# Four delta-rule heads computed on unnormalised keys and queries, with the next head's whole q projection moved ahead of the output transposes

## What is computed

```
conv = sum(src[:, j:j + T] * conv_w[j] for j in range(CONV_W))       # width 4, on q, k, v
qa, ka, va = jnp.split(jax.nn.silu(conv), 3, axis=-1)
qa = l2_normalize(qa) * HEAD_DIM_A ** -0.5
ka = l2_normalize(ka)
log_a = -exp(a_log) * softplus(a_raw + dt_bias);  beta = sigmoid(b_raw)
G = cumsum(g);  decay = exp(where(causal, G_i - G_j, -inf))          # per chunk
a_mat = where(strict, (k beta) @ k^T * decay, 0)
wu = triangular_solve(eye + a_mat, [k beta exp(G), v beta])
qk = (q @ k^T) * decay;  qg = q * exp(G);  kd = k * exp(G_last - G)
# scan over chunks
v_new = u - w @ S;  o = qg @ S + qk @ v_new;  S = S * g_last + kd^T @ v_new
o_a = rms_norm(o_a, gnorm_a) * silu(z)
```

## Time and profile before

| | us |
|---|---|
| median of 3 runs | 1989.44 |
| lowest, highest | 1988.54, 1991.89 |
| the profiled execution | 1989.23 |
| its span in the trace | 1987.2 |
| TensorE busy | 1910.3 |
| mean granted clock, share of full | 0.981 |

### The profile page before, as it was taken

How to read it: one execution, slowest core, us unless ns; L and a number is a source line. 1 busy time by engine, 2 the same in 40 slices (tenths; PEclk the granted TensorE clock), 3 DMA queues, 4 the chain that set the end, 5 groups by cost and what they waited for, 6 DMA issues and landing times.

```text
span 1987.2 us, 29633 instructions
## 1 busy us (share of the span) xinstructions
PE 1910.3 (96%) x12298; PEld 1855.4 (93%) x12298; DVE 755.8 (38%) x1525; ACT 619.8 (31%) x1335; POOL 559.3 (28%) x332
## 2 busy tenths in 40 slices
PE   6899999999999999999989999999999999999998
PEld 6898998999999899988989999999999999999997
DVE  5552552552452312332346424641252145115413
ACT  5532342342342323334424323321231023103311
POOL 1241141131131110211114434531343234214431
PEclk9999999989999999999989999999999999999999
DMA  5312312312312432444554332221121122112212
GB/s 155 87 52 62 98 51 59 102 46 64 94 53 86 143 105 94 148 132 145 181 171 146 98 87 75 84 65 43 53 90 49 43 66 84 43 53 74 64 53 88
DMA packets 235839, 173.25 MB, mean 87 GB/s; under 512 B 16277, under 2 KB 225250, under 8 KB 235322
## 3 DMA queue, kind: packets, MB, share of 16 engines
q1 hardware_dynamic: 200586, 131.57, 22.4%
q10 hardware_dynamic: 35120, 39.80, 6.1%
HBM read 134.04 MB, written 47.72 MB: 91 GB/s over the span
## 4 chain that ended last, share of the span: by engine, by line
PE 81%; DVE 8%; ACT 4%; DMA 4%; issue 2%; POOL 1%; SPq 0%; DVEq 0%; ACTq 0%; POOLq 0%
PE dense L207 50%; PE dense L232 13%; PE work L1359 1%; PE work L1371 1%; PE work L995 1%; PE work L1005 1%; DVE systems L853 1%; PE work L1409 1%; PE work L207 1%; PE work L1392 1%; PE work L1351 1%; PE work L935 1%; PE work L1003 1%; PE work L962 1%; PE work L410 1%
## 5 line engine op out<-in xcount | busy, mean ns | idle before, releaser
L196 POOL TENSOR_TENSOR WL<-Wraw,WH 128x1024 fp32r<-128x1024 f32 (+1 forms) x131 | 315.3, 2407 | 1075.2 <-ACT WH L191 1075.1
L207 PE MATMUL dense<-hH,WH 128*128 128x352 f32 x1392 | 456.0, 328 | 5.5 <-POOL WL L196 5.5
L207 PE MATMUL dense<-hL,WH 128*128 128x352 f32 x1392 | 450.7, 324 | 0.0
L207 PE MATMUL dense<-hH,WL 128*128 128x352 f32 x1392 | 450.3, 324 | 0.0
L232 PE MATMUL dense<-hH,WH 128*128 128x352 f32 x744 | 268.8, 361 | 5.6 <-ACT fill L241 5.3
L207 PEld LDWEIGHTS dense<-hH,WH 128*128 128x128 f32 x1392 | 265.0, 190 | 6.9 <-POOL WL L196 5.7
L207 PEld LDWEIGHTS dense<-hL,WH 128*128 128x128 f32 x1392 | 265.1, 190 | 0.0
L207 PEld LDWEIGHTS dense<-hH,WL 128*128 128x128 f32 x1392 | 264.6, 190 | 0.0
L207 PE MATMUL dense<-gH,WH 128*128 128x352 f32 x768 | 247.5, 322 | 2.5 <-DVE gL L1754 1.7
L191 ACT ACTIVATE WH<-Wraw 128x1024 fp32r<-128x1024 f32 (+1 forms) x131 | 136.3, 1041 | 363.7 <-PE dense L207 296.3
L207 PE MATMUL dense<-gL,WH 128*128 128x352 f32 x768 | 247.8, 323 | 0.0
(11 more groups left out here) (318 smaller groups left out, 2652.0 us busy)
## 6 DMA issues: line engine op xcount, KB each, us to landing
Wraw<-in_w_in SPq DMA_DIRECT2D x51, 512.0 KB, 4.2
Wraw<-in_w_up SPq DMA_DIRECT2D x32, 512.0 KB, 4.0
Wraw<-in_w_down SPq DMA_DIRECT2D x32, 512.0 KB, 3.6
cache<-in_cache_win SPq DMA_DIRECT2D x20, 512.0 KB, 6.3
qkv_scratch<-fill ACTq DMA_DIRECT2D x54, 176.0 KB, 1.8
raw<-qkv_scratch SPq DMA_DIRECT2D x6, 1584.0 KB, 9.2
out_win_s<-in_cache_win ACTq DMA_DIRECT2D x16, 512.0 KB, 4.1
gb_scratch<-fill ACTq DMA_DIRECT2D x24, 176.0 KB, 2.5
```

Of the source, the lines that this page charges most:

```text
L196: G.tensor_tensor(WL[:, s, 0:k], Wraw[:, s, 0:k], WH[:, s, 0:k].bitcast(F32), ALU.subtract).then_inc(sem("w_split"), 1)
L207: ins = PE.matmul(out[:, 0:TN], w[:, s, k0 + k, :], x[:, k, cols], start=(k == 0 and i == 0), stop=(k == nk - 1 and i == 2))
```

## The change

Keys and queries stay unnormalised. kk and qk are taken from `qkv` itself, so nothing is transposed back: q is never transposed forward. The key norm enters as `rk2` (1 over the sum of squares, from ScalarE squares with accumulation over the transposed k in PSUM) in `at` and in the eviction of v_new, and as its root in `cvb` for v; q's norm enters at the end, in the output's mean (`qeps`, from nine one-column matmuls on `sqq`). exp(G) times q is made without transposes: ScalarE takes Exp of the broadcast `cum_b`, GpSimd multiplies by q (`qg`). Operations are regrouped: kbg and kd are made in 128x512 products from PSUM. All own jobs are issued as parts, the fills are dealt out anew, and for h < 3 the whole q projection (t = 0, 1, 2) of the next head stands ahead of the output transposes. The diff, cut:

```diff
 def head_tensor(pe, h):
-    for j in range(4):
-        for t in range(NG):
-            if j or (h and t):
-                job(pe, N_HEAD + j, N_HEAD + j + 8 * h, t)
...
-    fill_parts(0, 8)
...
+    proj(1, 0, 24)
+    proj(2, 0, 8)
+    if h == 0:
+        ab_tensor(pe)
+    proj(2, 8, 16)
+    pe.wait_ge(sem("silu"), 3 * h + 2)
+    pe.wait_ge(sem("oa_part"), 3 * h + 1)
+    for i, (lo, hi) in enumerate(((0, 4), (4, 8), (8, 9))):
+        for t in range(lo, hi):
+            c, n = tokens[t]
+            ins = PE.transpose(work[2 + i][0:n, P * (t - lo):P * (t - lo) + P], qkv[:, 1, c:c + n], ident[:, :])
+        ins.then_inc(sem("k_turned"), 1)
+    proj(2, 16, 24)
+    for i in (0, 1, 4, 2, 3):
+        if i == 4:
+            pe.wait_ge(sem("ev_v"), 3 * h + 3)
+            pe.wait_ge(sem("squared"), 3 * h + 3)
...
+            ins = PE.matmul(work[i][0:n, o:o + 2 * n].rearrange("p (x i) -> p x i", x=2), qkv[:, 1, c:c + n], qkv[:, 0:2, c:c + n], start=True, stop=True)
+    proj(3, 0, 17)
     pe.wait_ge(sem("conv_done"), 3 * h + 3)
+    pe.wait_ge(sem("at_made"), h + 2)
...
+    proj(3, 17, 21)
...
+    proj(3, 21, 24)
+    fill_parts(0, 8)
+    pe.wait_ge(sem("sq_q"), h + 1)
+    for t in range(NT9):
+        ins = PE.matmul(work[4][:, t:t + 1], sqq[:, P * t:P * t + P], ones[:, 0:1], start=True, stop=True)
+    fill_parts(8, 20)
-    fill_parts(27, 28)
+    fill_parts(20, 28)
-    fill_parts(28, 29)
+    fill_parts(28, 31)
-    fill_parts(29, 72)
+    fill_parts(31, 44)
-        fill_parts(72 + 2 * s, 73 + 2 * s)
+        fill_parts(44 + 4 * s, 46 + 4 * s)
-        fill_parts(73 + 2 * s, 74 + 2 * s)
+        fill_parts(46 + 4 * s, 48 + 4 * s)
-    scanned = (80, 83, 86, 88, 90, 92, 94, 96)
+    scanned = (60, 65, 69, 74, 78, 83, 87, 92)
-    job(pe, N_HEAD, N_HEAD + 8 + 8 * h, 0)
+    for t in range(NG if h < NH - 1 else 1):
+        job(pe, N_HEAD, N_HEAD + 8 + 8 * h, t)
     pe.wait_ge(sem("o_normed"), h + 1)
-def back(pe, h, t):
...
 def head_pool(pool, h):
...
+    pool.wait_ge(sem("silu"), 3 * h + 1)
+    G.tensor_tensor(qg[:], qg[:], qkv[:, 0], ALU.mult).then_inc(sem("emb_made"), 1)
+    pool.wait_ge(sem("at_made"), h + 2)
...
+    lvl(0)
+    lvl(1)
+    split(5)
+    pool.wait_ge(sem("v_turned"), 3 * h + 3)
+    lvl(2)
 def head_scalar(act, h):
+    def exps():
+        act.wait_ge(sem("e_arg"), h + 1)
+        A.activation(qg[:], cum_b[:], ACT.Exp)
...
 def head_vector(dve, h):
+    conv_of(0)
+    if h:
+        decays()
+    else:
+        ab_rows(dve)
+    conv_of(1)
...
+    for t, (c, n) in enumerate(tokens):
+        ins = V.scalar_tensor_tensor(out=at[0:n, t, 0:n], in0=x, scalar=rk2[0:n, t:t + 1], in1=emb[0:n, t, 0:n], op0=ALU.mult, op1=ALU.mult)
+    ins.then_inc(sem("at_made"), 1)
+    conv_of(2)
```

More of the change, by code:

```diff
@@ L572, in head_sync @@
                 sp.dma_start(sc_in[24:28, j, :], a["conv_w"][0][:, bass.ds(j * WA + h * HD, HD)]).then_inc(sem("sc_loaded"), 16)
-            for j in range(2, 6):
+            for j in range(2, 4):
                 load(j)
@@ L602, in split @@
                 split_lo(pool, N_HEAD + j, N_HEAD + j + 8 * h)
-            for j in range(2, 6):
-                split(j)
+            split(2)
+            if h == 0:
+                split(3)
+                split(4)
             pool.wait_ge(sem("e_ready"), h + 1)
@@ L658, in head_scalar @@
[L658 to L665, removed]
@@ new lines, in head_scalar @@
+            if h:
+                for t in range(NG):
+                    q_out(act, h, 0, t)
+            split(2)
+            q_out(act, h, 1, 0)
+            q_out(act, h, 1, 1)
+            if h:
+                exps()
+            q_out(act, h, 1, 2)
+            split(3)
+            silu(act, h, 0)
+            if h == 0:
+                ab_rows_out(act)
+            else:
+                act.wait_ge(sem("ss_done"), h)
+            act.wait_ge(sem("silu"), 3 * h + 1)
+            A.activation(sqq[:, 0:T], qkv[:, 0, :], ACT.Square).then_inc(sem("sq_q"), 1)
@@ new lines, in head_scalar @@
+            q_out(act, h, 2, 2)
+            split(4)
+            act.wait_ge(sem("mean"), NT9 + 2 * h + 1)
+            A.activation(nk[:], ssk[:], ACT.Sqrt).then_inc(sem("root"), 1)
+            act.wait_ge(sem("oa_part"), 3 * h + 1)
+            for t in range(NG):
+                done(act, N_HEAD + 3 + 8 * h, t)
+                A.activation(silz[:, TN * t:TN * t + TN], dense[t][:, 0:TN], ACT.Silu).then_inc(sem(f"d_free{t}"), 1)
+                if t == 0:
+                    silu(act, h, 2)
@@ L763, in head_vector, with conv_of @@
                 V.memset(pre[:, s, 0:3], 0.0)
-            for j in range(3):
+            def conv_of(j):
                 s = j % 2
@@ L925, in head_tensor, with proj @@
-            fill_parts(0, 8)
+            def proj(j, first, last):
+                for p in range(first, last):
+                    part(pe, N_HEAD + j, N_HEAD + j + 8 * h, p)
+            pe.wait_ge(sem("sc_loaded"), 96 * h + 96)
+            pe.wait_ge(sem("s0_new"), h + 1)
+            pe.wait_ge(sem("ab_read"), 3)
+            apart(pe)
+            for x in range(3):
+                ins = PE.transpose(work[4][:, 28 * x:28 * x + 28], sc_in[:, x], ident[0:28, 0:28])
+            ins.then_inc(sem("sc_turned"), 1)
@@ L930, in head_tensor @@
             ins.then_inc(sem("tails_turned"), 1)
-            pe.wait_ge(sem("squared"), 2 * h + 2)
-            for x in range(2):
-                for t in range(NT9):
-                    ins = PE.matmul(work[4][:, NT9 * x + t:NT9 * x + t + 1], sq[:, x, P * t:P * t + P], ones[:, 0:1], start=True, stop=True)
+            proj(3, 17, 21)
+            pe.wait_ge(sem("silu"), 3 * h + 3)
+            for i, (lo, hi) in enumerate(((0, 4), (4, 8), (8, 9))):
+                for t in range(lo, hi):
+                    c, n = tokens[t]
+                    o = P * (t - lo) if i < 2 else P
+                    ins = PE.transpose(work[(0, 1, 4)[i]][0:n, o:o + P], qkv[:, 2, c:c + n], ident[:, :])
+                ins.then_inc(sem("v_turned"), 1)
```

310 lines of the change are left out of this document (134 added, 176 removed).

## The result

The changed kernel takes 2019.09 us (median of 4 executions, 2016.89 to 2019.82) against 1988.99 of the kernel before: ratio 1.0149, 95% interval 1.0131 to 1.0166. It is slower by 1.5%, +30 us where I forecast +5, and above my range. Its profiled execution has a span of 2015.0 us, 27.8 more than before.

The account below looks back on a forecast made before the run. TensorE, busy for 96% of the span, was taken as the bound. Removed work and old clock drops against new waits and clock drops gave +4.9 each in heads one and three, +2.5, -6.6; taken as +5: 1994.2 us, range 1970 to 2008.

Parts of the forecast that it names:

- What is removed: Per head: dropped transposes, one-column matmuls, five waits, block changes and short scan pauses save 12.0 us.
- kk's fifth group: In kk, TensorE waits until VectorE and ScalarE have read transposed k from the banks it writes: +1.8 us.
- The turn: Between heads, TensorE waits for dense bank 0, freed by the first eviction of q: +1.8 us.
- The chain to the k transposes: TensorE waits at the k transposes for Silu of k, delayed by VectorE and GpSimd taking turns: +7.1 us.
- u 41.1: Forecast end of Silu of k, 41.1 us after the previous head's last L1055 matmul.
- conv(2): Third convolution, behind at and taking turns with GpSimd's levels, makes TensorE wait at the tails transposes: +4.5 us.
- K: Start of the k transposes; from it TensorE's dense work was forecast done at +16.8, the third convolution at +21.3.
- The clock: One 3.4 us half-speed stretch behind each of two long waits a head: +3.4 us a head, +1.7 in head zero.
- rival D: Low-clock stretches behind the new waits are long ones of 6.8 us: +11.9, 2006.1 us; chance 0.15.
- A: VectorE and GpSimd do not take turns, so waits at k and tails transposes shrink: 1963.5 us; chance 0.18.
- B: Clock stays up behind the new waits, seven low stretches fewer: -11.9, 1982.3 us; chance 0.15.
- C: The solve's inverse comes later than TensorE wants it; a 10 us slip per head gives 2008 us; chance 0.05.

Follow-up runs that it names:

- e5: Changed kernel, but in heads one to three GpSimd splits weight tile 3 first and holds its em, emb, qg chain until Silu of k: 2000.2 us (1.0058).
- e4: Changed kernel, but in heads one to three ScalarE runs Silu of q ahead of the last eviction of k and the Exps: 1994.13 us (1.0024).
- e2: Changed kernel, but in head zero GpSimd splits weight tile 4 behind its chain of masks instead of ahead of it: 2017.63 us (1.0141).
- e3: Changed kernel, but VectorE runs the third convolution (v) ahead of the kk products and at operations: 1995.35 us (1.0032).
- e6: Changed kernel with 54 extra matmuls of 352 columns ahead of the k transposes in each of heads one to three: 2017.35 us (1.0143).
- e9: e7 with TensorE's own v and z projection parts moved ahead into its waits, same instructions in another order: 1963.12 us (0.9856).
- e7: Changed kernel with the edits of e2, e3 and e4, and only the first third of q ahead of the output transposes: 1973.95 us (0.9931).

## Why the prediction was wrong

The direction and the three places were right, the size was not: +30 for +5. In head one the forecast was +4.9 and the measured +10.2. The 5.3 between them are 3.3 at the k transposes, 2.5 of low clock, 0.8 less removed, 0.5 at the other two waits, less 1.8 for a wait that was none. Over heads one to three this makes 15.1, and head zero came out 10.0 above its forecast (+3.4 for -6.6). By its own steps:

- **What is removed, -12.0.** About right. Head one is longer by 10.2. The waits above stand for 10.4 + 4.9 + 1.9 = 17.2 and the low clock for 5.9 against 1.7 before; 17.2 + 4.2 - 10.2 leaves 11.2 for what was removed. It is less than the sum says in part because the wait at the first merge stayed (0.5 at L1047). The 1.8 that I booked for kk's fifth group was no wait in heads one to three: TensorE's waits there hold none at L993.
- **The turn, +1.8.** It measured 1.9. What I left out is the low stretch of 3.4 us behind it, under full work, 1.7.
- **The chain to the k transposes, +7.1: the main step that failed.** It measured 10.4, and TensorE came 1.7 later too; Silu of k ended 5.1 us later in the head than my u 41.1. I had conv(1) start when Silu of q was done, at u 32.0, and "four passes and four long operations take turns". The two tail copies ahead of the passes, which I had counted 0.6 in conv(0) and nothing here, cannot start before the last eviction of k; GpSimd's chain, begun just ahead of its end, held them until u 33.4: 1.4. And turns were not taken one for one: the passes and L814 took 11.5 us and not 7.8, because one pass sat through two GpSimd operations and GpSimd also had a weight split in the row, so five long operations and not four. e5 shows what the hold costs: without it the wait is 2.9 to 3.6 and the kernel 19 us faster. e4 shows that it was ScalarE's order that put the two side by side.
- **conv(2), +4.5.** It measured 4.9 in heads one to three, but not as I had it. The passes did not take turns with GpSimd's levels (4.10 for the three, which is free); the two tail copies in front of them were held, for 2.37 and 2.34. And both ends of the wait came over 2 us later than forecast: TensorE at K + 19.0 for 16.8, the convolution at K + 23.8 for 21.3. So the near number is in part luck. In head zero the wait is 13.2: the prediction gave it the same 4.5, and overlooked that GpSimd has the split of tile 4 in front of its mask chain there. The Exps that the chain needs are done at 85.5, but ScalarE makes the high part for that split only behind the last eviction of v, and the split ran from 90.64. With 2.0 for 0.45 at the k transposes and a longer low stretch the forecast for head zero, -6.6, became +3.4. e2 shows this cause, but gained no more than 1.5 us, since the time went into kk's wait. e3, which shortens the same wait to 5.3, makes head zero 5.8 shorter (its last L1109 matmul ends at 198.29 and not 204.35, its first dense one starts at 55.53 and not 55.80).
- **The clock, +3.4 a head.** It measured 5.9 in head one; the old stretch at the one-column matmuls (1.7) went, as forecast. I took the 3.4 us stretch of before as the size; at waits of 5 to 13 us the stretches are 6.8 to 13.7 long (3.4 once, in head three). They begin inside the wait, so a good part costs nothing: rival D's 6.8 everywhere would have been too much for the same reason. e6 shows, in two heads of three, that the long stretch at the k transposes goes when the idle array is filled, and that 2.1 us of low clock ahead of another wait are worth less than 1.
- **Rivals.** A (the two engines do not take turns) is refuted by e5: VectorE is held; B (no low clock) by the rows above; C did not happen, no wait for the inverse from HBM shows.

The upper bound of 2008 fell because the large misses had one sign: I priced each lock and stretch at the shortest that the trace of before showed, and took GpSimd's chain to start free in head zero. Only kk's wait (1.8 a head) and the part behind the heads (3.7) went the other way.

## What to carry to other kernels

A kernel whose TensorE is 96% busy has its small matmuls covered by an order; 28 us less work for TensorE was worth nothing while the reordering put two chains of other engines, ScalarE's Exps and VectorE's convolution, in front of it. Walk the longest chain of the new order through all engines, and keep long GpSimd operations off the stretch in which VectorE is that chain: holding GpSimd back gained 19 us here. Fewer instructions paid only after the order was mended (e9, 1.4% under the kernel before).

## What the runs showed of the hardware

- Short VectorE operations are held beside GpSimd's as long ones are. Copies of 3 and 24 columns a partition, 0.17 and 0.18 us in e5, took 1.8 to 2.6 in the changed kernel; a product of nine columns took 2.34 in e2 and 0.16 in the changed kernel. The Trainium skill (SBUF — State Buffer, SBUF: two separate sides) names a VectorE operation in a fast mode or with two SBUF inputs as what locks against GpSimd, by whole instructions; these agree with it, and being short is no protection.
- A copy of three columns took 6.15 us in e7, through the rest of one GpSimd operation and two more that followed without a gap. In the changed kernel such a copy (L807) was through at the end of the first one, with the next close behind. What decides between the two cases no run shows.
- VectorE's reads of PSUM beside the same chain were not held: in e5 the products of the transposed k (L852, which is L850 in the changed kernel) take 0.69 and 0.68 beside em and emb, the same as without.
- The stretches of low clock in heads zero to three of the changed kernel came in lengths of 3.4, 6.8, 10.2 and 13.7 us. Those at the k and the tails transposes begin while TensorE stands idle, except that of head three's tails transposes, and run on for 3.4 to 5.3 us of its next work. That at the turn begins about 1 us behind a wait of 1.9, under full work. In e9 the one that is left begins behind one-column matmuls.
- More work can be free: 162 extra matmuls of 352 columns (54 in each of three heads) did not lengthen the kernel, since they lay in a wait of 10.4 us.
